# Conditioning rows of the first block: the matrix by rows in 8 KB lines, part of the contraction on DVE, the rest on PE

## The chip, the cores and the metric

The kernel runs on one core of one Trainium2 chip. The metric is the device time of one execution in microseconds (us), the median of three runs. A time "in the span" is counted from the first instruction of the profiled execution.

## What is computed

Three blocks of a network run one after the other over 512 tokens of width 1024. The change lies in the first step of the first block: a condition vector `c` of 1024 numbers goes through SiLU, is multiplied by a matrix `w_ada` of 1024 x 6144 (25.17 MB in float32), and a bias is added. The result is six rows of 1024 numbers, with which the tokens are shifted, scaled and gated:

```python
c_act = jax.nn.silu(c)                       # c: [1, 1024]
mod = c_act @ w_ada[l] + b_ada[l]            # w_ada: [1024, 6144], b_ada: [6144]
shift1, scale1, gate1, shift2, scale2, gate2 = jnp.split(mod, N_MOD, axis=-1)
h = modulate(rms_norm(x, norm1_g[l]), shift1, scale1)    # h * (1 + scale) + shift
...
x = x + gate1[:, None, :] * (merged @ w_out[l])
h2 = modulate(rms_norm(x, norm2_g[l]), shift2, scale2)
x = x + gate2[:, None, :] * peer(h2, ...)
```

All the rest (the mixers, the expert layer, the second and third block) stays as it is.

## The kernel before, in words

The program is a row of stages. `stage` (L42) opens a block in which each of the five engines runs its own list of instructions, ordered against the others by semaphores alone; at its end all engines meet (L45, L49) before the next stage begins. So nothing of the next stage starts before the slowest engine of this one is done.

`adaptive_rows` (L496) is the first real stage, called by `block_one` (L1104). The next one is the first norm of the tokens, whose first instruction on DVE (VectorE) is the BATCH_NORM_STATS of L399. The result of `adaptive_rows` is `mod`, six rows of 1024 numbers, each repeated on all 128 partitions.

- **Tiles.** The matrix is taken in 12 chunks of 512 columns. A chunk comes in two pieces of 1 MB (`kmajor`, L56), each with 4 of the 8 groups of 128 input rows: 128 partitions x 4 lines of 2 KB. A ring of `SLOTS` = 4 slots of 1 MB over the buffer `h_features` takes the 24 pieces.
- **SP** issues the pieces in order (L510), each after PE has used the slot's last piece, and then the first two 1 MB pieces of the next weights into `ring_raw` (L93).
- **ACT** (ScalarE) issues the load of `c` as a column (4 KB), the load of the bias repeated on all partitions straight into `mod` (3 MB written), computes SiLU, and after the 3rd and 6th chunk issues the loads of two gain rows (`row_a`, `row_b`, 0.5 MB each, repeated) and of the tokens `x` (2 MB).
- **PE** (TensorE) makes the product. `c_rep` holds SiLU(c) repeated over 128 columns, so that each of the 8 matmuls of a chunk (L536, 128x128 by 128x512, float32) adds up one group of 128 input rows, and the sum comes out alike on all 128 partitions. Two PSUM banks are used in turn. A float32 matmul shows as two records in the trace.
- **DVE** repeats SiLU(c) once (L545), adds each chunk's PSUM bank to `mod` (L551), and at the end forms (1 + scale) * gain for rows 1 and 4 (L555).

In the names of the trace `ada_ring` is the ring, `in_w_ada` the matrix in memory, `row_a` and `row_b` the gains, SPq and ACTq the DMA issues of an engine, PEq and DVEq an engine's sequencer (branches, drains).

Of the kernel before, what the change touches and what calls it, by code (L numbers as in the profile page):

```python
# [19 lines left out]
ALU = mybir.AluOpType  # L20
AX = mybir.AxisListType

P = 128
SEQ = 512
NT = SEQ // P
D = 1024
KD = D // P
BANK = 512
# [4 lines left out]
SLOTS = 4  # L33
# [461 lines left out]

def adaptive_rows(nc, core, d, mod, norm1_gain, norm2_gain):  # L496

    chunks = 6 * D // BANK
    pieces = [half for j in range(chunks) for half in kmajor(d["w_ada"][0], j * BANK, BANK)]
    ring = over(nc, core.hT_whole, "ada_ring", [P, SLOTS, PIECE])  # L500
    with buffers(nc, c_col=[P, KD], c_silu=[P, KD], c_rep=[P, KD, P]) as (c_col, c_silu, c_rep), \
            stage(nc, "ada", "c_loaded", "bias_loaded", "rest_loaded", "silu_done", "c_ready", "multiplied", "used", "evacuated",
                  *[f"landed{n}" for n in range(SLOTS)]) as (
                block, c_loaded, bias_loaded, rest_loaded, silu_done, c_ready, multiplied, used, evacuated, *landed):
        @block.sync
        def _(sp):
            for n, src in enumerate(pieces):
                if n >= SLOTS:
                    sp.wait_ge(used, n - SLOTS + 1)
                sp.dma_start(ring[:, n % SLOTS, :].rearrange("p (k n) -> p k n", k=KD // 2), src).then_inc(landed[n % SLOTS], 16)  # L510
            load_ahead(core, sp, core.splits + 2)

        @block.scalar
        def _(act):
            act.dma_start(c_col[:], d["c_col"]).then_inc(c_loaded, 16)
            act.dma_start(mod[:].rearrange("p a f -> p (a f)"), d["b_ada"][0, :].partition_broadcast(P)).then_inc(bias_loaded, 16)
            act.wait_ge(c_loaded, 16)
            nc.scalar.activation(c_silu[:], c_col[:], ACT.Silu).then_inc(silu_done, 1)
            act.wait_ge(multiplied, 3)
            act.dma_start(norm1_gain, d["norm1_g"][0, :].partition_broadcast(P)).then_inc(rest_loaded, 16)  # L520
            act.dma_start(norm2_gain, d["norm2_g"][0, :].partition_broadcast(P)).then_inc(rest_loaded, 16)
            act.wait_ge(multiplied, 6)
            act.dma_start(core.x[:], d["x"].rearrange("b (t p) f -> p (b t) f", p=P)).then_inc(rest_loaded, 16)

        @block.tensor
        def _(pe):
            pe.wait_ge(c_ready, 1)
            for c, turn, odd, _ in pairs(pe, 0, chunks):
                pe.wait_ge(evacuated, c + 1)
                for half in range(2):  # L530
                    slot = 2 * odd + half
                    pe.wait_ge(landed[slot], 16 * (turn + 1))
                    w = ring[:, slot, :].rearrange("p (k n) -> p k n", k=KD // 2)
                    for k in range(KD // 2):
                        kk = half * KD // 2 + k
                        mm = nc.tensor.matmul(core.ps[:, odd, :], c_rep[:, kk, :], w[:, k, :], start=kk == 0, stop=kk == KD - 1)  # L536
                    mm.then_inc(used, 1)
                    if half == 1:
                        pe.drain().then_inc(multiplied, 1)

        @block.vector
        def _(dve):
            dve.sem_inc(evacuated, 2)
            dve.wait_ge(silu_done, 1)
            nc.vector.tensor_copy(c_rep[:], c_silu[:].unsqueeze(2).to_broadcast([P, KD, P])).then_inc(c_ready, 1)  # L545
            dve.wait_ge(bias_loaded, 16)
            rows = mod[:].rearrange("p a f -> p (a f)")
            for j, _, odd, _ in pairs(dve, 0, chunks):
                dve.wait_ge(multiplied, j + 1)
# [1940 lines left out]
def column_tiles(v):  # L2490

    return np.ascontiguousarray(v.reshape(-1, P).T)
# [43 lines left out]
```

## Time and profile before

| | |
|---|---|
| median of 3 runs | 5344.36 us |
| lowest and highest of the 3 | 5342.21 and 5353.56 us |
| profiled execution, its own time | 5340.43 us |
| its span in the trace | 5338.6 us |
| start of the first norm's first DVE instruction in the span | 112.10 us |
| PE busy over the span | 4357.7 us (82%) |
| matrix loads of the stage | 24 of 1 MB |
| mean granted clock of PE over the span | 0.909 |

The granted clock (PEclk) is a share of full speed: 1.00 is the level of 2.4 GHz, 0.50 that of 1.2 GHz. "GB/s" is what all 16 DMA engines moved in a stretch. A timeline row has its start, its length, and in brackets how long the engine had been idle and what released it. The changed stage takes the first 112 us; the other stages have the same instructions before and after.

### The profile page before, as it was taken

How to read it: one execution, taken by the hardware profiler on the slowest of the kernel's cores; microseconds unless marked ns; L12 is line 12 of the kernel's file. 1: busy time of each engine (PE TensorE's matmuls, PEld its weight loads, DVE VectorE, ACT ScalarE, POOL GpSimd, SP SyncE). 2: the span in 40 equal slices, each digit the busy share in tenths (PEclk: the TensorE clock that was granted, in tenths of full speed). 3: DMA queues.
4: the chain of work that ended last, by engine and by line, in shares of the span. 5: the costliest groups of instructions: out<-in, count | busy, mean ns of one | idle time of the engine just before them, and what ended most of it. 6: DMA issues, size and time to landing. Idle time of an engine off the chain costs nothing. (4 is left out here: it accounts for less than half of the span.)

```text
span 5338.6 us, 46516 instructions
## 1 busy us (share of the span) xinstructions
PE 4357.7 (82%) x16256; PEld 2946.5 (55%) x16256; DVE 3132.0 (59%) x5411; ACT 731.9 (14%) x1680; POOL 818.7 (15%) x756
## 2 busy tenths in 40 slices
PE   7788969787787777677978678699996789787987
PEld 3676755222222222446746446577775567576876
DVE  2344357778778775654464485555556246445774
ACT  0111111111111010110131341100001210311000
POOL 1000023434433343100020041100002000001001
PEclk9899989999999999888989779799998699588998
DMA  7212216999999999200201101122222022022222
GB/s 252 85 56 81 88 63 260 423 424 423 423 416 416 415 416 421 76 24 8 75 16 64 49 1 53 60 87 89 91 90 68 24 75 80 8 73 74 95 77 75
DMA packets 212434, 813.26 MB, mean 152 GB/s; under 512 B 20288, under 2 KB 22608, under 8 KB 146448
## 3 DMA queue, kind: packets, MB, share of 16 engines
q0 software_dynamic: 73728, 536.90, 24.2%
q1 hardware_dynamic: 137408, 267.62, 15.1%
q10 hardware_dynamic: 1104, 6.30, 0.3%
q8 instruction: 104, 1.70, 0.1%
q14 instruction: 90, 0.74, 0.0%
HBM read 808.67 MB, written 2.10 MB: 152 GB/s over the span
## 5 line engine op out<-in xcount | busy, mean ns | idle before, releaser
L122 DVE CAST ring_high<-ring_raw 128x2048 fp32r<-128x2048 f32 (+2 forms) x250 | 274.4, 1097 | 934.7 <-PE psum L152 864.8
L150 PE MATMUL psum<-h_features,ring_high 128*128 128x512 f32 (+3 forms) x1432 | 566.0, 395 | 56.8 <-DVE ring_low L124 25.0
L151 PE MATMUL psum<-h_features,ring_high 128*128 128x512 f32 (+3 forms) x1432 | 562.4, 393 | 0.0
L152 PE MATMUL psum<-h_features,ring_low 128*128 128x512 f32 (+3 forms) x1432 | 562.0, 392 | 0.0
L124 DVE TENSOR_TENSOR ring_low<-ring_raw,ring_high 128x2048 fp32r<-128x2048 f32 (+2 forms) x250 | 509.6, 2038 | 19.0
L150 PE MATMUL psum<-ring_high,h_features 128*128 128x512 f32 x1120 | 443.1, 396 | 59.1 <-DVE ring_low L124 45.6
L925 PE MATMUL psum<-slots_ring,evacuation_tmp 128*128 128x512 f32 x816 | 403.7, 618 | 104.8 <-DVE evacuation_tmp L1023 104.7
L151 PE MATMUL psum<-ring_low,h_features 128*128 128x512 f32 x1120 | 441.0, 394 | 0.0
L152 PE MATMUL psum<-ring_high,h_features 128*128 128x512 f32 x1120 | 440.6, 393 | 0.0
L417 POOL TENSOR_SCALAR mean_var<-mean_var 128x1 f32<-128x1 f32 (+3 forms) x43 | 10.3, 241 | 2710.2 <-DVEq L455 1500.5
L925 PE MATMUL psum<-slots_features,evacuation_tmp 128*128 128x512 f32 x612 | 302.1, 617 | 77.2 <-DVE evacuation_tmp L1023 77.0
L925 PEld LDWEIGHTS psum<-slots_ring,evacuation_tmp 128*128 128x128 f32 x816 | 138.4, 189 | 369.0 <-DVE evacuation_tmp L1023 269.4
L150 PEld LDWEIGHTS psum<-h_features,ring_high 128*128 128x128 f32 (+3 forms) x1432 | 265.4, 185 | 130.0 <-issue 53.1
L1055 DVE CUSTOM_DVE_ANT_0 slots_ring<-slots_ring,h_tokens 128x1024 f32<-128x1024 f32 x204 | 249.8, 1225 | 101.5 <-DMA slots_ring<-in_peer_uv,expert 98.2
L152 PEld LDWEIGHTS psum<-h_features,ring_low 128*128 128x128 f32 (+3 forms) x1432 | 265.1, 185 | 64.4 <-issue 0.9
L151 PEld LDWEIGHTS psum<-h_features,ring_high 128*128 128x128 f32 (+3 forms) x1432 | 265.5, 185 | 62.5 <-issue 0.6
L150 PEld LDWEIGHTS psum<-ring_high,h_features 128*128 128x128 f32 x1120 | 213.6, 191 | 108.1 <-issue 48.3
L1096 ACT ACTIVATE weight<-score 128x1 f32<-128x1 f32 x512 | 103.9, 203 | 1131.9 <-DVE score L1055 1131.7
L872 POOL DMA_INDIRECT slots_ring<-in_peer_uv,expert x204 | 208.6, 1023 | 323.0 <-PE psum L925 291.2
L925 PEld LDWEIGHTS psum<-slots_features,evacuation_tmp 128*128 128x128 f32 x612 | 104.0, 189 | 274.2 <-DVE evacuation_tmp L1023 199.1
L925 PE MATMUL psum<-slots_mod,evacuation_tmp 128*128 128x512 f32 x416 | 207.5, 623 | 57.7 <-DVE evacuation_tmp L1023 57.6
L152 PEld LDWEIGHTS psum<-ring_high,h_features 128*128 128x128 f32 x1120 | 213.5, 191 | 45.1
(453 smaller groups left out, 7227.0 us busy)
## 6 DMA issues: line engine op xcount, KB each, us to landing
ring_raw<-in_w_in SPq DMA_DIRECT2D x94, 1024.0 KB, 5.0
ring_raw<-in_w_gate_up SPq DMA_DIRECT2D x32, 1024.0 KB, 5.1
ada_ring<-in_w_ada SPq DMA_DIRECT2D x24, 1024.0 KB, 5.9
ring_raw<-in_w_up_pairs SPq DMA_DIRECT2D x20, 1024.0 KB, 4.9
ring_raw<-in_w_down SPq DMA_DIRECT2D x33, 512.0 KB, 3.6
ring_raw<-in_w_out SPq DMA_DIRECT2D x12, 1024.0 KB, 5.0
ring_raw<-in_w_down SPq DMA_DIRECT2D x10, 1024.0 KB, 4.9
ring_raw<-in_peer_w_q SPq DMA_DIRECT2D x8, 1024.0 KB, 5.1
```

The costliest lines, as they stand in the source:

```text
L122: nc.vector.tensor_copy(high, whole)
L124: return nc.vector.tensor_tensor(low, whole, high.bitcast(F32), ALU.subtract)
L150: nc.tensor.matmul(out, a[0], b[0], start=start, stop=False)
L151: nc.tensor.matmul(out, a[0], b[1], start=False, stop=False)
L152: return nc.tensor.matmul(out, a[1], b[0], start=False, stop=stop)
L417: nc.gpsimd.tensor_scalar(v, v, eps, None, ALU.add).then_inc(done, 1)
L872: nc.gpsimd.indirect_dma_start(out=slots[slot_of[n]], out_offset=None, in_=rows, in_offset=bass.IndirectOffsetOnAxis(ap=expert[:, t, i:i + ...
L925: mm = nc.tensor.matmul(banks(t)[q], diagonal[:, n % DIAGONALS, :], slots[slot_of[n]][:, D + q * BANK:D + (q + 1) * BANK], start=i == 0, s ...
L1055: nc.vector.tensor_tensor_reduce(out=u, in0=u, in1=core.h[:, t, :], scale=1.0, scalar=0.0, op0=ALU.mult, op1=ALU.add, accum_out=score[:, i ...
L1096: nc.scalar.activation(weight[:, i:i + 1], score[:, i:i + 1], ACT.Gelu).then_inc(activated, 1)
```

## The change

The matrix is laid out anew in memory (`laid_out`): first by the six rows of the result, then by quarters of the contraction, then by partition. A piece is now 128 partitions x one line of 8 KB: 2 groups of 128 input rows by all 1024 columns of one row of `mod`. There are again 24 pieces of 1 MB, 4 for each row of `mod`, in the order of rows 1, 4, 0, 2, 3, 5. The ring has 8 slots, 4 over `h_features` and 4 over `ring_high` and `ring_low`.

Of the 4 pieces of a row, DVE takes the first three: 6 instructions of 128x1024 that multiply a group by its SiLU(c), a number per partition, and add it to `sums`. Each waits by a drain for the one before. PE takes the fourth piece as before (4 matmuls against `c_rep`), adds the bias by 2 matmuls over one partition of ones, and adds the 128 partitions of `sums` by 2 matmuls against a block of ones. So 8 matmuls remain for a row instead of 16. Rows 1 and 4 are brought from PSUM by DVE with their gain in one instruction each; the other four by a copy on ACT. The bias is loaded as one line of 24 KB, and the gains and `x` are issued by ACT after the first row's sums.

```diff
+ADA_ORDER = (1, 4, 0, 2, 3, 5)
+ADA_PIECES, ADA_SUMMED = 4, 3
...
         @block.sync
         def _(sp):
-            for n, src in enumerate(pieces):
-                if n >= SLOTS:
-                    sp.wait_ge(used, n - SLOTS + 1)
-                sp.dma_start(ring[:, n % SLOTS, :].rearrange("p (k n) -> p k n", k=KD // 2), src).then_inc(landed[n % SLOTS], 16)
+            for i, r in enumerate(ADA_ORDER):
+                for q in range(ADA_PIECES):
+                    if i >= turns:
+                        if q < ADA_SUMMED:
+                            sp.wait_ge(used_summed, ADA_SUMMED * (i - turns) + q + 1)
+                        else:
+                            sp.wait_ge(used_direct, i - turns + 1)
+                    sp.dma_start(ring(i, q), d["w_ada_rows"][r, q].rearrange("p (k n) -> p k n", k=2)).then_inc(landed_at(i, q)[0], 16)
             load_ahead(core, sp, core.splits + 2)
...
         def _(act):
-            act.dma_start(mod[:].rearrange("p a f -> p (a f)"), d["b_ada"][0, :].partition_broadcast(P)).then_inc(bias_loaded, 16)
+            act.dma_start(bias[:], d["b_ada"]).then_inc(bias_loaded, 16)
...
-            act.wait_ge(multiplied, 3)
+            act.wait_ge(summed, 1)
...
+            for i, r in enumerate(ADA_ORDER):
+                if r not in gains:
+                    act.wait_ge(multiplied, i + 1)
+                    nc.scalar.copy(mod[:, r, :].rearrange("p (b n) -> p b n", b=2), core.ps[:, bank(i):bank(i) + 2, :]).then_inc(copied, 1)
+            act.wait_ge(x_loaded, 16)
...
         def _(pe):
...
-                        mm = nc.tensor.matmul(core.ps[:, odd, :], c_rep[:, kk, :], w[:, k, :], start=kk == 0, stop=kk == KD - 1)
...
+                if i >= 4:
+                    pe.wait_ge(gained, gained_at[i - 4] + 1)
...
+                    nc.tensor.matmul(out[half], ones[0:1, :], bias[:, r * D + half * BANK:r * D + (half + 1) * BANK], start=True, stop=False)
+                pe.wait_ge(*landed_at(i, ADA_SUMMED))
+                for k in range(2):
+                    for half in range(2):
+                        mm = nc.tensor.matmul(out[half], c_rep[:, k, :], ring(i, ADA_SUMMED)[:, k, cols[half]], start=False, stop=False)
+                mm.then_inc(used_direct, 1)
+                pe.wait_ge(summed, i + 1)
+                for half in range(2):
+                    mm = nc.tensor.matmul(out[half], ones[:], sums[:, i % 2, cols[half]], start=False, stop=True)
+                mm.then_inc(multiplied, 1)
...
         def _(dve):
-                nc.vector.tensor_tensor(part, part, core.ps[:, odd, :], ALU.add).then_inc(evacuated, 1)
...
+            for i, r in enumerate(ADA_ORDER):
+                if i >= 2:
+                    dve.wait_ge(multiplied, i - 1)
+                total = sums[:, i % 2, :]
+                for q in range(ADA_SUMMED):
+                    dve.wait_ge(*landed_at(i, q))
+                    for k in range(2):
+                        c = c_silu[:, 2 * q + k:2 * q + k + 1]
+                        if q + k == 0:
+                            done = nc.vector.tensor_scalar(total, ring(i, q)[:, k, :], c, None, ALU.mult)
+                        else:
+                            dve.drain()
+                            done = nc.vector.scalar_tensor_tensor(total, ring(i, q)[:, k, :], c, total, ALU.mult, ALU.add)
+                    done.then_inc(used_summed, 1)
+                    if q == 0 and i - 1 in gained_at:
+                        gain(i - 1)
+                dve.drain().then_inc(summed, 1)
```

On DVE, at the start of `adaptive_rows`, the program had this (the two L551 rows are the body of a loop that runs 6 times):

```order
L545 COPY c_rep<-c_silu 128x1024
L170 UNCONDITIONAL_BRANCH
L170 ISA
L551 ISA
L551 TENSOR_TENSOR mod<-mod,psum 128x512
L549 REGISTER_ALU
L551 ISA
L551 TENSOR_TENSOR mod<-mod,psum 128x512
L170 REGISTER_ALU
L170 COMPARE_AND_BRANCH
L555 SCALAR_TENSOR_TENSOR mod<-mod,row_a 128x1024
L555 SCALAR_TENSOR_TENSOR mod<-mod,row_b 128x1024
```

And has this now (`ada_features` and `ada_ring` are the two halves of the ring; L591 and L594 are the products, L577 the rows with a gain):

```order
L581 COPY c_rep<-c_silu 128x256
L591 TENSOR_SCALAR sums<-ada_features_83,c_silu 128x1024
L594 SCALAR_TENSOR_TENSOR sums<-ada_features_83,c_silu,sums 128x1024 x5
L591 TENSOR_SCALAR sums<-ada_ring_84,c_silu 128x1024
L594 SCALAR_TENSOR_TENSOR sums<-ada_ring_84,c_silu,sums 128x1024
L577 SCALAR_TENSOR_TENSOR mod<-psum,row_a 128x1024
L594 SCALAR_TENSOR_TENSOR sums<-ada_ring_84,c_silu,sums 128x1024 x4
L591 TENSOR_SCALAR sums<-ada_features_83,c_silu 128x1024
L594 SCALAR_TENSOR_TENSOR sums<-ada_features_83,c_silu,sums 128x1024
L577 SCALAR_TENSOR_TENSOR mod<-psum,row_b 128x1024
```

DVE has 36 products instead of 12 additions, and the two gains stand inside the second and third row instead of at the end.

On PE the same place, before (a loop of 6 turns, 16 matmuls each):

```order
L532 ISA
L536 MATMUL psum<-ada_ring_83,c_rep 128x512 x8
L529 REGISTER_ALU
L536 MATMUL psum<-ada_ring_83,c_rep 128x512 x8
L170 REGISTER_ALU
L170 COMPARE_AND_BRANCH
```

And now (the first two of six rows; L560 is the bias, L564 the fourth piece, L568 the sum over partitions):

```order
L560 MATMUL psum<-bias,ones 128x512 x2
L564 MATMUL psum<-ada_features_83,c_rep 128x512 x4
L568 MATMUL psum<-sums,ones 128x512 x2
L560 MATMUL psum<-bias,ones 128x512 x2
L564 MATMUL psum<-ada_ring_84,c_rep 128x512 x4
L568 MATMUL psum<-sums,ones 128x512 x2
```

PE has 48 matmuls in the stage instead of 96, written out without a loop; those of L568 stand behind DVE's sums.

## Rows read from the trace of the kernel before

**Rows 1.** the page, its head: engine, busy us, share of the span, instructions.
```profile
PE 4357.7 (82%) x16256; PEld 2946.5 (55%) x16256; DVE 3132.0 (59%) x5411; ACT 731.9 (14%) x1680; POOL 818.7 (15%) x756
```
**Rows 2.** busy time by stretch; last three columns: PEclk, DMA share, GB/s.
```profile
50.00:60.00 10.00, 9.60 (x23) 4.08 (x22) 0.69 (x1) 0.00 (x0) 0.00 (x0) 1.00 0.93 300
80.00:90.00 10.00, 9.60 (x23) 4.02 (x23) 0.69 (x1) 0.00 (x0) 0.00 (x0) 1.00 0.87 300
```
**Rows 3.** waits of the first 145 us: engine, line, releaser: us, times, longest.
```profile
DVE mod L551 <- PEq L539: 93.6, 12, 16.9
PE psum L536 <- DMA ada_ring<-in_w_ada: 12.9, 2, 8.3
PE psum L536 <- issue: 6.0, 11, 0.7
```
**Rows 4.** by line, first 160 us: busy us, mean ns of one.
```profile
L536 PE MATMUL psum<-ada_ring,c_rep 128*128 128x512 f32 x192 | 89.1, 618 | 18.9 <-DMA ada_ring<-in_w_ada 12.9 <-issue 6.0
L551 DVE TENSOR_TENSOR mod<-mod,psum 128x512 f32 x12 | 8.2, 687 | 93.6 <-PEq L539 93.6
```
**Rows 5.** timeline, end of the stage: start us, us, engine, line, operation.
```profile
100.88 7.11 PE L536 MATMUL psum<-ada_ring,c_rep 128*128 128x512 f32 x16 [0.40 <-issue]
108.17 0.69 DVE L551 TENSOR_TENSOR mod<-mod,psum 128x512 f32 x1 [6.82 <-PEq L539]
108.97 1.22 DVE L555 SCALAR_TENSOR_TENSOR mod<-mod,row_a 128x1024 f32<-128x1024 f32 x1
112.10 1.29 DVE L399 BATCH_NORM_STATS2 bn_parts<-x_tokens 128x6 f32<-128x512 f32 x2 [0.76 <-PEq L49]
```
**Rows 6.** DMA issues, first 200 us: KB each, median us to landing.
```profile
ada_ring<-in_w_ada SPq DMA_DIRECT2D x24, 1024.0 KB, 5.9
ring_raw<-in_w_in SPq DMA_DIRECT2D x8, 1024.0 KB, 5.2
x_tokens<-in_x ACTq DMA_DIRECT2D x1, 2048.0 KB, 10.9
```
**Rows 7.** busy time by stretch, for the DMA rate in the last column.
```profile
3.00:5.00 2.00, 0.00 (x0) 0.00 (x0) 0.00 (x0) 1.28 (x1) 0.00 (x0) 1.00 0.62 128
8.00:12.00 4.00, 3.66 (x5) 1.62 (x6) 0.00 (x0) 0.00 (x0) 0.00 (x0) 1.00 1.00 426
16.00:18.00 2.00, 0.00 (x0) 0.00 (x0) 0.00 (x0) 0.00 (x0) 0.00 (x0) 1.00 1.05 397
1000.00:1100.00 100.00, 78.59 (x160) 26.95 (x160) 78.77 (x197) 13.70 (x46) 40.06 (x40) 1.00 1.01 424
1900.00:2000.00 100.00, 78.66 (x160) 26.75 (x158) 76.04 (x189) 10.71 (x42) 40.77 (x40) 1.00 1.01 414
```
**Rows 8.** groups by line and form on DVE, whole span.
```profile
L318 DVE SCALAR_TENSOR_TENSOR evacuation_tmp<-psum,taps,evacuation_tmp 128x511 f32<-128x511 f32 x21 | 15.8, 750 | 3.4 <-issue 3.4
L1222 DVE TENSOR_SCALAR y<-y,mean_var 128x128 f32<-128x128 f32 x32 | 6.4, 287 | 6.1 <-POOL mean_var L419 6.1
L1222 DVE TENSOR_SCALAR y<-y,mean_var 128x256 f32<-128x256 f32 x16 | 4.3, 350 | 3.5 <-POOL mean_var L419 3.5
L1055 DVE CUSTOM_DVE_ANT_0 slots_ring<-slots_ring,h_tokens 128x1024 f32<-128x1024 f32 x204 | 249.8, 1225 | 101.5 <-DMA slots_ring<-in_peer_uv,expert 98.2
```
**Rows 9.** timeline on PE, and PEclk by stretch behind two of the gaps.
```profile
18.34 5.40 PE L536 MATMUL psum<-ada_ring,c_rep 128*128 128x512 f32 x8 [4.57 <-DMA ada_ring<-in_w_ada]
...
4392.71 0.50 PE L150 MATMUL psum<-ring_high,yT 128*128 128x512 f32 x1 [3.33 <-DVEq L243]
...
4393.00:4396.40 3.40, 3.40 (x16) 2.74 (x16) 3.32 (x2) 0.00 (x0) 0.00 (x0) 1.00 0.02 5
...
2765.42 1.79 PE L1649 MATMUL psum<-q_tile,far 128*128 128x128 f32 x11 [3.60 <-DVE far L1556]
...
2765.70:2769.00 3.30, 3.30 (x21) 3.30 (x20) 2.97 (x5) 0.00 (x0) 0.00 (x0) 0.61 0.03 7
```
**Rows 10.** groups by line and form on ACT, whole span.
```profile
L2212 ACT COPY y<-psum 128x1024 f32<-128x1024 f32 x4 | 4.0, 1014 | 7.9 <-PE psum L2205 7.9
```

More of the change, by code:

```diff
@@ L32 @@
 PIECE = KD // 2 * BANK
-SLOTS = 4
 ALPHA = 2.0 ** 0.25
@@ L493, with _ @@
 SGU_GROUPS, SGU_DIM = 4, 256
+ADA_ORDER = (1, 4, 0, 2, 3, 5)
+ADA_PIECES, ADA_SUMMED = 4, 3
 def adaptive_rows(nc, core, d, mod, norm1_gain, norm2_gain):
[L498 to L504, printed above, removed]
+    turns = 2
+    gains = {1: norm1_gain, 4: norm2_gain}
+    gained_at = {i: n for n, i in enumerate(i for i, r in enumerate(ADA_ORDER) if r in gains)}
+    in_features = over(nc, core.hT_whole, "ada_features", [P, ADA_PIECES, 2, D])
+    in_ring = over(nc, core.high, "ada_ring", [P, ADA_PIECES, 2, D])
+    ring = lambda i, q: (in_features, in_ring)[i % turns][:, q]
+    with buffers(nc, c_col=[P, KD], c_silu=[P, KD], c_rep=[P, 2, P], ones=[P, P], sums=[P, 2, D], bias=[1, 6 * D]) as (
+            c_col, c_silu, c_rep, ones, sums, bias), \
+            stage(nc, "ada", "c_loaded", "bias_loaded", "gains_loaded", "x_loaded", "ones_ready", "silu_done", "c_ready", "used_summed", "used_direct",
+                  "summed", "multiplied", "copied", "gained", *[f"landed{n}" for n in range(turns * ADA_PIECES)]) as (
+                block, c_loaded, bias_loaded, gains_loaded, x_loaded, ones_ready, silu_done, c_ready, used_summed, used_direct,
+                summed, multiplied, copied, gained, *landed):
+        bank = lambda i: 2 * (i % 4)
+        landed_at = lambda i, q: (landed[ADA_PIECES * (i % turns) + q], 16 * (i // turns + 1))
+        @block.gpsimd
+        def _(pool):
+            nc.gpsimd.memset(ones[:], 1.0).then_inc(ones_ready, 1)
@@ L527, in _ @@
             pe.wait_ge(c_ready, 1)
-            for c, turn, odd, _ in pairs(pe, 0, chunks):
-                pe.wait_ge(evacuated, c + 1)
-                for half in range(2):
[L531 to L535, printed above, removed]
-                        mm = nc.tensor.matmul(core.ps[:, odd, :], c_rep[:, kk, :], w[:, k, :], start=kk == 0, stop=kk == KD - 1)
-                    mm.then_inc(used, 1)
-                    if half == 1:
-                        pe.drain().then_inc(multiplied, 1)
+            pe.wait_ge(bias_loaded, 16)
@@ L541, in _ @@
         @block.vector
         def _(dve):
-            dve.sem_inc(evacuated, 2)
-            dve.wait_ge(silu_done, 1)
[L545 to L549, printed above, removed]
-                part = rows[:, bass.ds(j * BANK, BANK)]
-                nc.vector.tensor_tensor(part, part, core.ps[:, odd, :], ALU.add).then_inc(evacuated, 1)
@@ L552, in _, with gain @@
-            dve.drain()
-            dve.wait_ge(rest_loaded, 48)
-            for which, gain in ((1, norm1_gain), (4, norm2_gain)):
-                nc.vector.scalar_tensor_tensor(mod[:, which, :], mod[:, which, :], 1.0, gain, ALU.add, ALU.mult)
+            def gain(i):
+                r = ADA_ORDER[i]
+                dve.wait_ge(gains_loaded, 32)
+                dve.wait_ge(multiplied, i + 1)
+                nc.vector.scalar_tensor_tensor(mod[:, r, :].rearrange("p (b n) -> p b n", b=2), core.ps[:, bank(i):bank(i) + 2, :], 1.0,
+                                               gains[r].rearrange("p (b n) -> p b n", b=2), ALU.add, ALU.mult).then_inc(gained, 1)
```

13 lines of the change are left out of this document (9 added, 4 removed).

## The prediction

> **What bounds the kernel now.** I read the page's head first: PE is busy 4357.7 us of the span, 82% [rows 1]. That share is an average over the whole program; the change touches only the first 112 us, so I read that stretch alone. By stretches of 10 us, PE is busy 9.60 at a granted clock of 1.00, DVE 0.69, and the DMA engines move 300 GB/s [rows 2]. The waits say who is late: DVE waits 93.6 us for PE, while PE waits 12.9 us for the matrix, all of it in the first 19 us, and 6.0 us at the turn of chunks [rows 3]. So the stage is bound by PE: 192 records of 618 ns [rows 4], 16 of them (8 matmuls) in 7.11 us for a chunk [rows 5], which is 0.89 us for a float32 matmul at the 2.4 GHz level. The reader should see that the DMA engines, at 300 GB/s, are held back by the ring: a slot comes free only when PE has used it. Behind the last chunk stand DVE's addition and two gain instructions of 1.22 us, then 0.76 us of meeting, and the norm starts at 112.10 [rows 5]. The stages end in a meeting of all engines, so whatever this stage gives back moves the start of the norm by just that much.
>
> **The change, part by part.**
>
> *PE's matmuls.* 16 per row of `mod` become 8: 8 x 0.89 = 7.1 us for a row at 2.4 GHz, 43 us in all. PE stops being the bound if a row takes longer elsewhere.
>
> *DVE's products.* The trace has no 128x1024 product with a number per partition whose operands all lie in SBUF. Nearest: the gain instruction, 1.22 us [rows 5]; and at 128x511 the form with a number per partition takes 750 ns [rows 8], where an addition of two tensors over 512 takes 687 [rows 4], 0.06 more. So 1.28 us, and 0.10 for the drain, as between the end of L551 (108.17 + 0.69) and the next start (108.97) [rows 5]: 1.38. The first product of a row has one tensor only: 287 ns for 128 elements and 350 for 256 [rows 8], so 0.063 per 128 and about 0.73 for 1024, with its drain 0.85. A row costs DVE 0.85 + 5 x 1.38 = 7.75 us, 46.5 in all, and 2 x 1.3 for the gains. Does DMA at full rate slow DVE? A 128x1024 instruction in the gather stage takes 1225 ns [rows 8] beside 424 GB/s [rows 7]: no. Bounds of a product: 1.22 and 1.6.
>
> *DMA.* A row is four pieces, 4.19 MB. At what rate? Three rows bear on it. The 2 KB lines of this stage, with the ring not yet full, came at 397 GB/s; mixed with the 24 KB lines of the bias, 426; the gather of 8 KB lines later in the kernel at 424, and at 414 in a worse stretch [rows 7]. The new lines are 8 KB, so I take 424: 9.9 us for a row. That is more than PE's 7.1 and DVE's 7.75, so **the bound moves to DMA**. Eight slots hold 20 us of transfers ahead, which covers DVE's wait for the gains in the second row (they are issued only after the first row's sums) and the clock of PE.
>
> On this the Trainium skill speaks against the change: "DMA: Bandwidth & Descriptors" (section on bandwidth, "Where 436 GB/s comes from") says that for loads from memory the memory side, about 358 GB/s for a core, binds. The trace disagrees: 424 GB/s held for 100 us [rows 7]. By the page's figure, an estimate, the bytes below would take 78.4 us instead of 66.2, and the gain would be 19.7 us.
>
> *The end of the loads.* All bytes: 24 pieces 25.17 MB, `x` 2.10, gains 1.05, bias 0.02: 28.34 MB. The 3 MB of the repeated bias are gone. The first 2 us (3 to 5) moved 128 GB/s [rows 7], 0.26 MB. The remaining 28.08 MB at 424 GB/s take 66.2 us: last byte at 71.2. Between last byte and landing: a lone 1 MB lands 5.2 us after its issue [rows 6], of which 2.6 are its bytes at 397 GB/s. Of the other 2.6, before the first byte and behind the last, I put 0.8 behind (bounds 0 and 2.6). The last piece lands at **72.0**. The two pieces into `ring_raw` are issued behind it on the same queue; nobody needs them before the norm is over, so they cost nothing.
>
> *The tail.* The last piece of each row is PE's. DVE gets its third piece 2.5 us earlier and needs 2.8, so its sums are ready 0.3 to 0.7 us after the last landing, under PE's 4 direct matmuls (3.6 us). Then 2 matmuls for the sum: 6 x 0.89 = 5.3 us at 2.4 GHz, 10.7 at 1.2. Which? PE will have idled some 9.9 - 7.1 = 2.8 us before it. In the trace a gap of 4.57 us was followed by a stretch at half clock (8 records in 5.40 us instead of 3.6); one of 3.60 us by a mean clock of 0.61, one of 3.33 by 1.00 [rows 9]. So I add half the loss of the middle case: 0.9. Tail: 6.2. Then 0.2 to the reader (107.99 to 108.17), ACT's copy of 128x1024 from PSUM, 1.01 [rows 10], and the meeting, 0.76 [rows 5]. DVE has nothing behind PE's last matmul any more: its two gains are done in the rows before.
>
> **Sum:** 72.0 + 6.2 + 0.2 + 1.0 + 0.8 = 80.2, against 112.10: **31.9 us less**. Everything after is the same program. Against the profiled execution, 5340.4 - 31.9 = 5308.5; the median of the runs lies 3.9 above that execution, so 5344.4 - 31.9 = **5312.5**, which I give. The later stages' clock steps fall differently against the work once it all starts 32 us earlier; that may move the total by a few us either way.
>
> **The rivals.**
>
> 1. *The lines are served no better than 2 KB ones.* 28.08 MB at 397 GB/s take 70.7 us, 4.5 more; at 386, as low as such a mix might fall, 6.5 more: 5317 to 5319. For it: a load by the SP queue is not the gather. Against: the rate rises with the line in rows 7, 397 to 424 and 426. Chance 0.13.
> 2. *The queue serves its transfers together, not in turn.* Then the row's four pieces land at once, and with the two for `ring_raw`: landing 5 us later (2.1 MB at 424) and DVE's 7.75 us behind it instead of beside it, with 1.8 for the sum. The norm starts near 72.0 + 5.0 + 7.75 + 1.8 + 2.0 = 88.5: 5321. Against: a median of 5.9 us to landing for 1 MB with others under way [rows 6]. Chance 0.09.
> 3. *PE stays the bound at a low clock.* With 2.8 us idle in each row the clock could stay at the 1.2 GHz level: 14.2 us for a row. From the first row's end near 15 + 10.7, five more: 96.8, norm at 98.8, 5331. Against: at 14.2 us a row PE would no longer idle, and in steady work rows 2 show 1.00; behind the gap of 4.57 us the slow records had an end too, since all 8 took 5.40 us and not 7.1 [rows 9]. Chance 0.05.
> 4. *The memory side binds below the rate of rows 7.* This core would then stay between the 300 GB/s of rows 2 and 397. Midway, at 350, the 28.08 MB take 80.2 us, 14.0 more, and the gain is 17.9: 5326.5. Chance 0.03. At 300 they take 93.6 us, the norm starts at 107.6 and the gain is 4.5 us, no measurable change: chance 0.02. Against both: 424 GB/s over 100 us [rows 7].
>    This is the mechanism of the Trainium skill's sentence above; with its 358 GB/s, an estimate again, the time would be 5324.7.
> 5. *Slower: the transfers do not overlap.* If each waited for the one before to land, 24 x 5.2 us [rows 6] = 125 us; norm near 135.5, 23 us later: 5368. It decides from 4.2 us per transfer on: (112.1 - 2.3 - 8.2) / 24. Against: 397 GB/s in rows 7 with several queued, where a lone one has 1 MB in 5.2 us, 202 GB/s. Chance 0.02.
>
> **How the numbers follow.** The forecast has 0.66, and its own bounds are: rate 414 to 430 (2 us later, 1 earlier), tail 5.3 to 10.7 (1 earlier, 4.5 later), a product of 1.6 us (DVE's row 9.3, still under 9.9; less than 1 us on the tail), and some 5 us for the clock steps of later stages: 5303 to 5321. The range reaches on over rivals 1 and 2 with a few us of the same clock steps: 5302 to 5326, with 0.12 left out (rivals 3, 4 and 5) beside the forecast's own ends. About 0.2% or 11 us is what a measurement of this kernel can tell from no change. The forecast, rivals 1, 2, 3 and rival 4 at 350 GB/s all gain 13 us or more: 0.66 + 0.13 + 0.09 + 0.05 + 0.03 = 0.96 faster; 0.02 same (rival 4 at 300); 0.02 slower (rival 5).
>
> **What would show it.** Right: the norm's first DVE instruction near 80 us; 410 to 425 GB/s in the stretches between 10 and 70 us; PE's waits in the stage now for the ring, and DVE's for the ring, not for PE; products of about 1.28 us. Rival 1 shows as 390 GB/s, rival 2 as landings of 10 us and more with DVE's six products bunched at the end, rival 3 as PEclk near 0.5 from 20 to 90 us. The forecast is wrong if the norm starts early but the total does not follow, or if the products take over 1.7 us, where DVE's row passes 9.9 us and becomes the bound.

## The result, and the profile after

The changed kernel takes 5316.76 us in the median of 6 runs (5312.19 to 5324.9), the kernel before 5346.85 in 6 runs beside it: ratio 0.9945, with a 95% interval of 0.9933 to 0.9957, or 30 us less. Timed a second time, it was 5322.0 us (5 runs) against 5339.8 (11 runs): ratio 0.9966, interval 0.9952 to 0.9979, 18 us less. Both intervals lie below 1, so the kernel is faster, by 0.55% and 0.34% in the medians. The forecast was 5312.5 with a range of 5302 to 5326. Both medians lie in it; the second gain is little more than half of the one forecast, and where the rest went is told below. (The first 3 of the 6 runs of before are those of the table ahead.)

The changed stage itself did nearly what was forecast. The page's head and the first 110 us in stretches, as [rows 1] and [rows 2] (the last three columns are PEclk, the DMA share and GB/s):

```profile
PE 4341.9 (82%) x16160; PEld 2939.7 (55%) x16160; DVE 3162.5 (59%) x5435; ACT 736.6 (14%) x1684; POOL 825.5 (16%) x757
30.00:70.00 40.00, 33.46 (x60) 12.69 (x58) 31.87 (x28) 2.02 (x2) 0.00 (x0) 0.79 1.01 422
52.00:62.00 10.00, 9.18 (x17) 3.45 (x16) 7.24 (x7) 1.01 (x1) 0.00 (x0) 0.83 1.01 421
```

The DMA engines now run full, 422 GB/s over 40 us at a share of 1.01, where [rows 2] had 300. DVE is busy 7.2 us of the 10 from 52 to 62 and PE 9.2, at a clock of 0.83, where I had expected 7.1 us of work for each 9.9. Over the 40 us PE is busy 33.5, at 0.79: part of its busy time is the slower clock.

The waits of the stage, against [rows 3] (engine, line, releaser, then us in total, times, longest): each engine that works on the matrix now waits for the matrix.

```profile
DVE mod L577 <- DMA row_b<-in_norm_g: 8.8, 1, 8.8
PE psum L560 <- DMA bias<-in_b_ada: 8.4, 1, 8.4
PE psum L564 <- DMA ada_features<-in_w_ada_rows: 7.7, 3, 3.5
PE psum L564 <- DMA ada_ring<-in_w_ada_rows: 5.3, 3, 3.5
DVE sums L591 <- DMA ada_ring<-in_w_ada_rows: 5.2, 3, 2.1
```

The groups of the stage, against [rows 4] and [rows 8] (busy us, mean ns of one): a product of DVE takes 1284 ns, the first of a row 753.

```profile
L594 DVE SCALAR_TENSOR_TENSOR sums<-ada_ring,c_silu,sums 128x1024 f32<-128x1024 f32 x15 | 19.3, 1284 | 1.8 <-DMA ada_ring<-in_w_ada_rows 0.7
L591 DVE TENSOR_SCALAR sums<-ada_ring,c_silu 128x1024 f32<-128x1024 f32 x3 | 2.3, 753 | 5.2 <-DMA ada_ring<-in_w_ada_rows 5.2
L564 PE MATMUL psum<-ada_ring,c_rep 128*128 128x512 f32 x24 | 16.8, 869 | 5.3 <-DMA ada_ring<-in_w_ada_rows 5.3
```

And the end of the stage in time, against [rows 5]: the last row of `mod`, from DVE's first product to the norm.

```profile
65.46 0.75 DVE L591 TENSOR_SCALAR sums<-ada_ring,c_silu 128x1024 f32<-128x1024 f32 x1 [2.06 <-DMA ada_ring<-in_w_ada_rows]
67.95 5.38 DVE L594 SCALAR_TENSOR_TENSOR sums<-ada_ring,c_silu,sums 128x1024 f32<-128x1024 f32 x4 [0.37 <-DMA ada_ring<-in_w_ada_rows]
69.97 1.98 PE L560 MATMUL psum<-bias,ones 1*128 1x512 f32 x4
72.87 5.40 PE L564 MATMUL psum<-ada_ring,c_rep 128*128 128x512 f32 x8 [0.93 <-DMA ada_ring<-in_w_ada_rows]
78.11 1.88 PE L568 MATMUL psum<-sums,ones 128*128 128x512 f32 x4
80.03 1.01 ACT L546 COPY mod<-psum 128x1024 f32<-128x1024 f32 x1 [8.94 <-PE psum L568]
81.89 1.29 DVE L398 BATCH_NORM_STATS2 bn_parts<-x_tokens 128x6 f32<-128x512 f32 x2 [8.56 <-PEq L48]
```

DVE is done with its six products at 73.33, while PE has only begun its last four matmuls at 72.87, when their piece landed. They take 5.24 us, at first at full clock and then, from 74 to 77 us, at half (0.51 and 0.50). The norm starts at 81.89 instead of 112.10: 30.2 us earlier.

### The profile page after: what moved, and what is told of

It reads as the page before. It is cut to its first block and busy times, and to the rows that moved or that the text cites. A ratio compares the mean times of both kernels' runs of the same rounds, so it can differ in the third digit from the quotient of the medians.

```text
span 5318.9 us, 46309 instructions
## 1 busy us (share of the span) xinstructions
PE 4341.9 (82%) x16160; PEld 2939.7 (55%) x16160; DVE 3162.5 (59%) x5435; ACT 736.6 (14%) x1684; POOL 825.5 (16%) x757
## 5 line engine op out<-in xcount | busy, mean ns | idle before, releaser
L123 DVE TENSOR_TENSOR ring_low<-ring_raw,ring_high 128x2048 fp32r<-128x2048 f32 (+2 forms) x250 | 509.5, 2038 | 19.8 <-issue 1.0
```

The costliest lines, as they stand in the source:

```text
L123: return nc.vector.tensor_tensor(low, whole, high.bitcast(F32), ALU.subtract)
```

## The experiments

In each diff the lines are those of the changed kernel with `+` and `-` against it. "The norm" is the start of its first instruction on DVE; the stretches are those of each kernel's own trace. Experiments 1 to 10 are one profiled execution each, so they are read by their traces and not by their totals: single totals of the kernel before alone range from 5328.45 to 5355.74 us. Those of experiments 3 to 10, in the order of their numbers, are 5326.76, 5340.34, 5326.57, 5299.51, 5321.64, 5321.68, 5314.75 and 5321.39 us. Experiments 5 and 6 leave out part of the product.

**1 and 2. Both kernels once more, unchanged.**

> The kernel before once more, unchanged, to see what moves by itself. In the two profiled executions the changed kernel starts the norm 30.2 us earlier but ends its span only 19.7 us earlier; 8.7 us of the difference lie in the gated linear attention stage of the second block (from the load of w in in_gla_w to the load of in_gla_norm: 205.1 us before, 213.8 after) where PE's granted clock is 0.85 against 0.81. Theory A (that stage's clock falls by chance of timing, in either kernel): norm again at 112.1 us within 0.5, total within 5342 to 5356, and this stage not fixed at 205.1 but anywhere in 204 to 215. Theory B (the change itself slows that stage): norm at 112.1 and the stage again at 205.1 within 1 us.

> The changed kernel once more, unchanged. Theory A (chance of the clock): norm at 81.9 us within 0.5, total 5312 to 5325, the gated linear attention stage anywhere in 204 to 215 us. Theory B (the change slows that stage): norm at 81.9 and that stage again at 213.8 within 1 us.

The norm started at 110.98 us in the kernel before (1.12 earlier, where 0.5 was allowed) and at 80.51 in the changed one (1.38 earlier): 30.5 us apart, as the first pair. Totals were 5335.28 and 5312.82, the first under its range too. The attention stage took 206.4 us and 210.6. Theory B (205.1 and 213.8, within 1 us) missed both. Theory A allowed anything from 204 to 215, so it holds both without being shown by them. The passage behind experiment 12 comes back to it.

The changed kernel's tail shows what the norm's 1.4 us are: here the clock was full, and the last direct matmuls took 3.5 us instead of 5.2. A row earlier it had been low: PE idled 2.58 us, and the direct matmuls took 6.5.

```profile
60.00:70.00 10.00, 7.42 (x11) 3.07 (x11) 7.25 (x7) 0.00 (x0) 0.00 (x0) 0.66 1.01 421
62.86 6.71 PE L564 MATMUL psum<-ada_features,c_rep 128*128 128x512 f32 x8 [2.58 <-DMA ada_features<-in_w_ada_rows]
73.12 3.70 PE L564 MATMUL psum<-ada_ring,c_rep 128*128 128x512 f32 x8
80.51 1.28 DVE L398 BATCH_NORM_STATS2 bn_parts<-x_tokens 128x6 f32<-128x512 f32 x2 [7.25 <-PEq L48]
```

The changed kernel thus has at least two courses. In the three stretches of 10 us from 50 to 80 the clock was 0.83, 0.83 and 0.83 in the first execution, and 1.00, 0.66 and 1.00 here and again in experiment 12 (norm at 80.41). An experiment's norm is therefore to be held against 80.4 to 81.9, and against one end of that only where the tail took the same course.

**3. The matrix in lines of 2 KB.**

```diff
-    ...reshape(KD // 2, 2, P, 6, D).transpose(3, 0, 2, 1, 4)).reshape(6, KD // 2, P, 2 * D)
+    ...reshape(KD // 2, 2, P, 6, 2, BANK).transpose(3, 0, 1, 4, 2, 5)).reshape(6, KD // 2, 4, P, BANK)
-                    sp.dma_start(ring(i, q), d["w_ada_rows"][r, q].rearrange("p (k n) -> p k n", k=2))
+                    sp.dma_start(ring(i, q).rearrange("p k (h n) -> p (k h) n", h=2), d["w_ada_rows"][r, q].rearrange("a p n -> p a n"))
```

> The changed kernel with one thing undone: the matrix comes in lines of 2 KB (4 lines a partition in each 1 MB piece) instead of one line of 8 KB; split between DVE and PE, ring, order and bytes stay. Theory 1 (the stage is bound by the stream, and the rate follows the line): the 28.08 MB at 395 instead of 423 GB/s take 4.7 us more, the norm starts at 86.6 us, the stretches between 30 and 70 us show 385 to 400 GB/s. Rival (the line does not matter, the split gave all): norm at 81.9 within 0.5, 420 GB/s. Rival (the line gave most of the gain): norm past 100 us.

```profile
50.00:60.00 10.00, 8.01 (x15) 2.96 (x14) 6.99 (x7) 1.01 (x1) 0.00 (x0) 0.77 1.05 387
78.23 5.95 PE L564 MATMUL psum<-ada_ring,c_rep 128*128 128x512 f32 x8 [3.52 <-DMA ada_ring<-in_w_ada_rows]
```

387 GB/s at a full share, the last piece 5.4 us later (78.23 against 72.87), the norm at 87.80, 5.9 later than in the first execution; the other 0.5 us are slower direct matmuls. Theory 1 holds, with a rate at its lower edge: the line of 8 KB is worth 5 to 6 us of the 30.

**4. All of the product on PE, with the new layout, ring and loads.**

```diff
-                pe.wait_ge(*landed_at(i, ADA_SUMMED))
...
+                for q in range(ADA_PIECES):
+                    pe.wait_ge(*landed_at(i, q))
+                    for k in range(2):
+                        for half in range(2):
+                            mm = nc.tensor.matmul(out[half], c_rep[:, 2 * q + k, :], ring(i, q)[:, k, cols[half]], start=False, stop=2 * q + k == KD - 1)
```

> The changed kernel with DVE's part given back to PE: new layout, 8 KB lines, 8 slots, bias by matmul and late gains stay; all four pieces of a row are multiplied on PE (16 matmuls and 2 for the bias), no sums on DVE. Theory 1 (PE was the bound, and the split freed the stream): 108 matmuls at 0.89 us are 96 us behind the first landing near 8.4, so the norm starts at 106 to 109 us, DMA falls to about 270 GB/s between 30 and 90 us, PE is over 9.5 of 10 us busy at clock 1.00. Rival (layout and ring gave the gain): norm at 82 to 88 us.

```profile
60.00:70.00 10.00, 9.89 (x23) 4.00 (x22) 0.00 (x0) 1.01 (x1) 0.00 (x0) 1.00 0.68 242
80.00:90.00 10.00, 10.00 (x21) 4.20 (x20) 0.00 (x0) 0.00 (x0) 0.00 (x0) 0.83 0.73 286
45.88 15.70 PE L562 MATMUL psum<-ada_features,c_rep 128*128 128x512 f32 x32
63.59 14.00 PE L562 MATMUL psum<-ada_ring,c_rep 128*128 128x512 f32 x32
114.90 1.29 DVE L398 BATCH_NORM_STATS2 bn_parts<-x_tokens 128x6 f32<-128x512 f32 x2 [69.70 <-PEq L48]
```

PE is never idle from 8.36 us on, DMA falls to 242 to 286 GB/s, and the norm starts at 114.90, later than in the kernel before and 6 us above my bound: the product of a row takes 14.0 us in two rows and 15.7 or 15.8 in four, since the clock dipped there although PE had no gap. With all of the product on PE nothing is gained, so the gain needs the split, which frees the stream. That layout, ring and late gains are worth nothing by themselves is not shown: this kernel also has 12 matmuls for the bias on PE, 10.7 us at 0.89 each, about as much as PE's idle time shrank (18.9 us in [rows 4], 8.4 here).

**5. Half of DVE's products left out.**

```diff
-                    for k in range(2):
+                    for k in range(1):
                         c = c_silu[:, 2 * q + k:2 * q + k + 1]
```

> The changed kernel with half of DVE's products left out: of each of its pieces only the first group of 128 input rows is multiplied (18 instructions instead of 36), so the second, fourth and sixth eighth of the contraction are missing from the result. Loads and PE's work stay. Theory 1 (the stream is the bound and DVE hides under it): norm at 81.9 us within 0.5. Rival (DVE's chain of drained products is the bound): 18 products of 1.38 us less, 25 us, norm at 60 to 70 us as far as the stream allows, with the stream above 430 GB/s. DVE's wait for the gains in the second row stays.

```profile
30.00:70.00 40.00, 33.37 (x60) 12.77 (x58) 14.21 (x13) 2.02 (x2) 0.00 (x0) 0.79 1.02 422
81.92 1.29 DVE L398 BATCH_NORM_STATS2 bn_parts<-x_tokens 128x6 f32<-128x512 f32 x2 [10.17 <-PEq L48]
```

DVE 14.2 us busy instead of 31.9 in the same 40 us, the stream at the same 422 GB/s, the norm at 81.92. The execution took the course of the first one (clock 0.83 in the tail), and its norm lies within 0.03 us of it: DVE's work is hidden.

**6. A quarter of the matrix less.**

```diff
-                for q in range(ADA_PIECES):
+                for q in (0, 1, 3):
...
-                for q in range(ADA_SUMMED):
+                for q in range(2):
```

> The changed kernel without the third piece of each row: neither loaded nor multiplied (6 of 24 pieces, 6.29 MB; the fifth and sixth eighth of the contraction are missing). DVE has 4 products a row, PE its 8 matmuls. Theory 1 (stream bound at 423 GB/s): 14.9 us less, norm at 67.0 us, if PE at 7.4 us of stream a row does not take over: its 8 matmuls are 7.1 us at clock 1.00 and more at the mean clock 0.83 now seen (about 8.6), in which case 6 rows of 8.6 from 15 us on give 67 to 70. Rival (PE or DVE bound now): norm at 78 us or later.

```profile
40.00:50.00 10.00, 9.64 (x19) 3.46 (x17) 6.59 (x6) 1.01 (x1) 0.00 (x0) 0.83 1.01 421
59.14 3.70 PE L564 MATMUL psum<-ada_ring,c_rep 128*128 128x512 f32 x8
66.45 1.29 DVE L398 BATCH_NORM_STATS2 bn_parts<-x_tokens 128x6 f32<-128x512 f32 x2 [8.42 <-PEq L48]
```

The norm at 66.45: 15.4 us less than in the first execution, where 6.29 MB at 422 GB/s are 14.9. That the two agree so well is partly luck: the last direct matmuls start only 13.7 us earlier (59.14 against 72.87), and the other 1.7 us are their full clock; against the executions with a full clock in the tail the norm gains 14.0. PE is 9.64 us of 10 busy here and works without a gap from 42.93 on, so its last direct matmuls did not wait for their piece. With 3.15 MB or 7.5 us of stream for a row, PE and not the stream sets the pace of the last two rows.

**7 and 10. PE kept busy between rows,** first with a second pair of bias matmuls over one partition, then with the same length of work over all partitions.

```diff
-                for half in range(2):
-                    nc.tensor.matmul(out[half], ones[0:1, :], bias[...], start=True, stop=False)
+                for stop in (True, False):
+                    for half in range(2):
+                        nc.tensor.matmul(out[half], ones[0:1, :], bias[...], start=True, stop=stop)
```

```diff
+                for half in (0, 1, 0, 1):
+                    nc.tensor.matmul(out[half][:, 0:2 * P], ones[:], c_rep[:].rearrange("p a n -> p (a n)"), start=True, stop=True)
```

> The changed kernel with two more matmuls a row on PE: the bias pair is done twice, the first time into the same banks and then overwritten, while PE would wait for the matrix; result unchanged. It asks whether PE's short idle time between rows (2.8 us of 9.9) costs clock in the tail. Now PEclk is 0.83 in each row, the last 4 direct matmuls take 5.24 us (72.87 to 78.11) instead of 3.6. Theory 1 (idling cost 1.7 us in the tail): with 8.9 us of work in 9.9, PEclk 1.00 between 50 and 80 us, last direct matmuls in 3.6 us, norm at 80.2. Rival (the clock falls all the same, or the additional work makes PE late): norm at 81.9 or later, up to 83.7.

> What fell in e7 was the clock in spite of a busy PE: over 9.9 of 10 us busy, PEclk 0.83 and 0.75, and the direct matmuls behind the four bias matmuls over one partition took 5.2 to 6.5 us instead of 3.6. Here the additional work has the same length (about 1.8 us a row), but as four matmuls over all 128 partitions and 256 columns; result unchanged. Theory C (it is the matmuls over one partition, not idle time, behind which the clock falls): with full-height work beside them PEclk is 0.95 or more between 50 and 80 us, the last direct matmuls take 3.6 to 3.8 us and the norm starts at 80 to 81 us. Theory D (the additional work as such makes PE late): norm at 84 to 86 us as in e7, PEclk 0.75 to 0.85.

Stretches of 10 us and the end of each kernel's stage in time: above the dots experiment 7, below them 10:

```profile
50.00:60.00 10.00, 10.00 (x20) 3.81 (x19) 7.24 (x7) 1.01 (x1) 0.00 (x0) 0.83 1.02 419
70.00:80.00 10.00, 10.00 (x18) 3.75 (x17) 4.33 (x4) 1.01 (x1) 0.00 (x0) 0.75 0.74 280
71.99 4.24 PE L561 MATMUL psum<-bias,ones 1*128 1x512 f32 x8
76.16 6.51 PE L565 MATMUL psum<-ada_ring,c_rep 128*128 128x512 f32 x8
86.28 1.29 DVE L398 BATCH_NORM_STATS2 bn_parts<-x_tokens 128x6 f32<-128x512 f32 x2 [11.71 <-PEq L48]
...
50.00:60.00 10.00, 10.00 (x30) 5.23 (x29) 6.39 (x6) 1.77 (x2) 0.00 (x0) 1.00 1.01 419
60.00:70.00 10.00, 8.94 (x20) 3.73 (x19) 7.24 (x7) 0.26 (x1) 0.00 (x0) 0.83 1.02 424
70.00:80.00 10.00, 10.00 (x27) 4.57 (x25) 4.06 (x4) 1.01 (x1) 0.00 (x0) 1.00 0.73 278
74.58 3.70 PE L566 MATMUL psum<-ada_ring,c_rep 128*128 128x512 f32 x8
81.90 1.29 DVE L398 BATCH_NORM_STATS2 bn_parts<-x_tokens 128x6 f32<-128x512 f32 x2 [7.59 <-PEq L48]
```

In experiment 7 PE is busy 10.00 us of 10 and the clock is 0.83 and 0.75; the last direct matmuls, behind four of the bias, take 6.5 us, and the norm starts at 86.28, 4.4 later than in the changed kernel. So PE had not idled before the clock fell: my theory of the tail, in the prediction and in this expectation, is refuted as far as idle time is its whole cause. In experiment 10 the clock is 1.00 in two of three stretches and 0.83 in the third, and the last direct matmuls take 3.5 us, but they start 1.7 us late behind the added work: 81.90. Theory C's 0.95 missed, and neither edit buys time. Nor do the two separate the theories: 1.00, a low stretch and 1.00 is also the course of the unchanged kernel in experiments 2 and 12. More telling for matmuls over one partition is experiment 4: without a gap ahead of them three of its six rows ran 1.7 us slow behind such a pair, and the kernel before, which has none, shows 1.00 in every stretch of 10 us from 30 to 100. But two rows of experiment 4 did not slow down, and no run took the bias off PE, so it is not shown.

**8. PE's piece first in each row.**

```diff
-                for q in range(ADA_PIECES):
+                for q in (3, 0, 1, 2):
```

> The changed kernel with the order of the pieces in each row turned: PE's piece is loaded first, DVE's three behind it. Theory (the tail is what follows the last landing): behind it now stand 4 matmuls and 2 more (5.24 and 1.9 us); then it is 2 products of 1.38 us and a drain, 2.9, and 2 matmuls of 1.8 to 2.7 after an idle time: norm at 79.0 to 80.5 us, 1.5 to 3 us earlier. Rival (DVE is too late with its pieces, for each row now needs 7.7 us of it in the last 7.4 us of the stream): norm at 81.9 or later.

```profile
69.86 3.70 PE L564 MATMUL psum<-ada_ring,c_rep 128*128 128x512 f32 x8
75.96 1.99 PE L568 MATMUL psum<-sums,ones 128*128 128x512 f32 x4 [2.40 <-DVEq L598]
79.84 1.29 DVE L398 BATCH_NORM_STATS2 bn_parts<-x_tokens 128x6 f32<-128x512 f32 x2 [3.98 <-PEq L48]
```

The direct matmuls are over at 73.6, PE waits 2.4 us for DVE's sums, and the norm starts at 79.84, 2.1 us earlier than in the first execution and within the expectation, but only 0.6 us earlier than in the executions whose tail also had the full clock (80.51 and 80.41). So the order of the last pieces is worth 0.6 to 2.1 us.

**9. The tokens behind the matrix,** issued by SP and no longer by ACT.

```diff
                     sp.dma_start(ring(i, q), ...).then_inc(landed_at(i, q)[0], 16)
+            sp.dma_start(core.x[:], d["x"].rearrange("b (t p) f -> p (b t) f", p=P)).then_inc(x_loaded, 16)
...
-            act.dma_start(core.x[:], d["x"].rearrange("b (t p) f -> p (b t) f", p=P)).then_inc(x_loaded, 16)
```

> The changed kernel with the load of the tokens x (2.10 MB) moved from ACT's queue, where it runs beside the second and third row of the matrix, to SP's queue behind the last piece of the matrix. Theory 1 (the stage is bound by what the stream moves before the last piece): 2.10 MB at 423 GB/s less ahead of it, 5.0 us; the last direct matmuls start at 67.9 instead of 72.87 and the norm at 75.5 to 77.0 us; x lands near 73 under the tail. Rival (the stream has slack, or x is now late): norm at 79 us or later.

```profile
67.58 5.33 PE L564 MATMUL psum<-ada_ring,c_rep 128*128 128x512 f32 x8 [1.13 <-DMA ada_ring<-in_w_ada_rows]
76.53 1.29 DVE L398 BATCH_NORM_STATS2 bn_parts<-x_tokens 128x6 f32<-128x512 f32 x2 [8.49 <-PEq L48]
```

The last piece is in use at 67.58 instead of 72.87 and the norm starts at 76.53: 5.4 us for 2.10 MB moved out of the way, with a tail of the same course (5.2 us for the last direct matmuls in both); 2.10 MB at 422 GB/s are 5.0. Together with experiments 3 and 5 this shows that the stage goes at the pace of the stream. PE is close behind: in experiments 2 and 12 its last direct matmuls no longer waited for their piece.

**11. The edits of experiments 8 and 9 together, timed, and 12. the changed kernel timed beside it.**

> The changed kernel with both edits that paid: PE's piece first in each row (e8: norm at 79.84 instead of 81.89, 2.1 us) and x behind the matrix (e9: 76.53, 5.4 us). If the stream is the bound up to its last piece and the tail follows it, the two add up: norm at 74.0 to 75.0 us, and the time falls by 7 us against the changed kernel, 37 us (0.7%) against the kernel before, ratio 0.993. Rival (x, which lands near 73 us, now holds up the end of the stage through ACT's wait): norm at 75 to 76 us. Rival (what the stage gives is lost later to the clock of the gated linear attention stage): norm at 74.5 but no gain over the changed kernel in the time.

> The changed kernel, unchanged, timed on the same chip as e11 for the comparison of the two: ratio to the kernel before 0.9935 to 0.9955 (30 us). Norm at 80.5 to 81.9 us. If the gated linear attention stage costs the changed kernel 4 to 9 us in every execution, the ratio lies near 0.996 instead.

```profile
45.00:50.00 5.00, 3.63 (x9) 1.12 (x7) 4.54 (x5) 0.00 (x0) 0.00 (x0) 1.00 0.75 265
30.75 1.23 DVE L577 SCALAR_TENSOR_TENSOR mod<-psum,row_a 128x1024 f32<-128x1024 f32 x1 [8.32 <-DMA row_b<-in_norm_g]
37.56 3.55 PE L568 MATMUL psum<-sums,ones 128*128 128x512 f32 x4 [11.64 <-DVEq L598]
76.57 1.29 DVE L398 BATCH_NORM_STATS2 bn_parts<-x_tokens 128x6 f32<-128x512 f32 x2 [3.98 <-PEq L48]
```

The two edits did not add up. The norm starts at 76.57, 2 us later than the sum of them would give (74.5). The row of the stretch 45 to 50 us shows where: 265 GB/s at a share of 0.75, so the stream paused. 5 us at 265 instead of 422 GB/s are 0.79 MB, or 1.9 us, and that is the 2. What stopped it is a slot that came free late. The trace has the chain: DVE waits 8.32 us for the gains in the second row (the changed kernel has this too, 8.8), its sums are late, PE waits 11.64 us for them, so its direct matmuls of the third row run from 42.95 to 46.65, and at 46.68 SP issues the piece that goes into their slot. Experiment 8 has the same chain, but there the stream still had the tokens to move, and it stayed at 419 GB/s from 45 to 50 us. No run took the wait for the gains away, so that this would give the 2 us back is argued and not shown. It is neither rival that I had written down. The medians: 5318.68 us (6 runs, 5301.68 to 5324.1), ratio 0.9960 (0.9947 to 0.9974), against 5322.0 and 0.9966 (0.9952 to 0.9979) for the changed kernel: no difference that this timing can tell. The profiled execution of experiment 11, 5301.68 us, is the fastest of its six, 17 us under their median.

**Where the rest of the time goes.** In its three profiled executions the norm of the changed kernel starts 29 to 32 us before those of the kernel before, but the totals give less: the first profiled pair (5340.43 and 5320.66) lies 19.8 us apart where the norms lie 30.2, and experiments 1 and 2 lie 22.5 apart where the norms lie 30.5. The gated linear attention stage of the second block, whose instructions are the same in all of them, takes these times (the stretch of the row, from the load of `in_gla_w` to that of `in_gla_norm`; in order: before, before in experiment 1, after, experiment 11; its columns are those of the stretches above):

```profile
2628.27:2833.39 205.12, 167.33 (x732) 115.02 (x732) 110.00 (x147) 59.30 (x138) 41.77 (x33) 0.86 0.08 24
2625.39:2831.75 206.36, 168.55 (x732) 118.02 (x732) 109.90 (x147) 59.30 (x138) 41.66 (x33) 0.85 0.08 24
2596.92:2810.74 213.82, 176.81 (x732) 121.58 (x732) 106.88 (x147) 59.30 (x138) 42.08 (x33) 0.82 0.08 23
2585.31:2787.67 202.36, 167.01 (x732) 115.03 (x732) 109.80 (x147) 59.31 (x138) 42.70 (x33) 0.86 0.08 25
```

205.1, 206.4, 213.8 and 202.4 us. The busy time of ACT and POOL is alike; PE has the same 732 records, and is busy 167 to 169 us at a clock of 0.85 or 0.86, 177 at 0.82. The stage is slower where the clock is lower. Over all profiled executions it took 205.1 to 206.4 us in the kernel before (two executions) and with all of the product on PE (once), 209.5 to 213.9 in ten of those with the split, and 202.4 in experiment 11. So part of the gain is given back there in ten of eleven profiled executions with the split, by 3 to 9 us: of the 10.4 us that the first pair lost behind the norm, 8.7 are this stage. (Experiments 1 and 2: 4.3 of 8.0.) The rest lies in later stages that I did not separate. Two profiled executions of the kernel before are few, however. Over all runs of the first timing the medians lie 30.1 us apart, as far as the norms do; the first pair lies closer because the kernel before was profiled 6.4 us under its median and the changed one 3.9 over its own. How long the stage takes in the runs without a trace is not known. It is not a fixed price of the change: the same kernel had 210.6 and 213.8, experiment 11 had the least of all (in the fastest of its six runs), and experiments 4 and 11 differ from the changed kernel in the first 115 us alone. What in those first microseconds decides how the clock falls 2.5 ms later stays open; I have no run that separates it.

## Why the prediction came out as it did

- **What bounds the kernel before.** Right: PE. Experiment 4 puts its work back and the stage is again as long as before and a little longer (114.90 against 112.10), with PE never idle.
- **DVE's products.** Forecast 1.28 us and 0.73, measured 1.284 and 0.753; a row takes 7.87 us (65.46 to 73.33) against 7.75. The end of the stage does not wait for it (experiment 5).
- **The stream.** Forecast 424 GB/s, measured 422; the last piece was to land at 72.0 and PE was released by it at 72.87. The 422 holds for 30 to 70 us; from 5 to 72 us the trace has 419, since the stretch from 20 to 30 came at 402. At 419 the 28.08 MB take 0.8 us more than at 424. The first 2 us (3 to 5) moved 214 GB/s and not 128, which is worth 0.4 us the other way. The remaining 0.5 I can't place: the landing, for which I had put 0.8 with bounds of 0 and 2.6, is not to be read by itself. Rival 1 is what experiment 3 builds: 2 KB lines come at 387 GB/s, within the 386 to 397 of its price, and cost 5.9 us where 4.5 to 6.5 were worked out. The Trainium skill's 358 GB/s ("DMA: Bandwidth & Descriptors", section on bandwidth, "Where 436 GB/s comes from") does not bind here: the matrix itself came at 422. I had read that passage alone: ahead of it the same section of the Trainium skill gives about 358 GB/s as what each core gets when both cores of a pair stream, and this kernel runs on one core; no run here has two.
- **The tail.** This term was mis-sized, and its reason was at best half right. Forecast 6.2 us; measured 7.1 in the profiled execution (72.87 to 79.99) and 5.4 in the other two (73.12 to 78.54 in experiment 2). So 6.2, a loss halved for not knowing, lies between two courses, and that it is close to their middle is luck. I had PE idle 2.8 us in each row. In the first execution it was busy 9.2 us of 10 in the last rows at a clock of 0.83, and the gap ahead of the last direct matmuls was 0.93 us; in experiments 4 and 7 the clock fell with no gap. In experiments 2 and 12 a gap of 2.6 us did precede the slow direct matmuls of the fifth row, as I had reasoned, and PE then had no gap, and the full clock, ahead of the last ones. Rival 3 has a grain of truth in it: PE at this clock is nearer to the bound than I thought, as experiment 6 shows.
- **Behind the tail.** Copy 1.01 as forecast, the way to it 0.04 instead of 0.2, the meeting 0.85 instead of 0.76.
- **The sum.** 80.2 forecast; 81.89, 80.51 and 80.41 measured in the three profiled executions of the changed kernel. A gain of 31.9 us in the stage was forecast; 30.2 and 30.5 measured in the two pairs. The kernel before moved too: its norm started at 112.10 and at 110.98.
- **"Everything after is the same program."** The instructions are, the time is not. I allowed 5 us for the clock steps of later stages; the attention stage alone moved by up to 8.7 between the two profiled executions I compare, so this term was too small for a single execution. That the second timing (18 us) falls short for the same reason is likely and not shown, since the runs of a timing leave no trace.
- **The total.** The median of 5316.76 is 4.3 above the forecast. Of this, 2.5 are the kernel before, whose median is 5346.85 over six runs and was 5344.36 over the three that I had. The gain, 30.1 by the medians, is 1.8 short of the 31.9, and the stage's own gain was short by 1.7 in the first pair. In the second timing the gain is 14 short, and I can't say by which stage. My own sign of a wrong forecast, a norm that starts early with a total that does not follow, is thus met in part there (18 us of about 30) and in the first profiled pair (19.8 of 30.2).
- **The bounds.** The widths that I gave my own terms (2 us later or 1 earlier for the rate, 4.5 or 1 for the tail, under 1 for the products, 5 either way for later stages) add up to 5305.5 and 5325, not to the 5303 and 5321 that I wrote. The range of 5302 to 5326 covers both.
- **Signs I had named.** "Landings of 10 us and more" was a poor sign for rival 2: the median landing is 16 us simply because eight transfers stand in the queue, and the pieces still arrive in turn:

```profile
ada_features<-in_w_ada_rows SPq DMA_DIRECT2D x12, 1024.0 KB, 16.2
55.55 0.75 DVE L591 TENSOR_SCALAR sums<-ada_features,c_silu 128x1024 f32<-128x1024 f32 x1 [2.08 <-DMA ada_features<-in_w_ada_rows]
58.02 5.38 DVE L594 SCALAR_TENSOR_TENSOR sums<-ada_features,c_silu,sums 128x1024 f32<-128x1024 f32 x4 [0.35 <-DMA ada_features<-in_w_ada_rows]
```

  DVE waits 2.08 us for the first piece of a row and 0.35 for the second; bunched landings would show one long wait and six products without any.

## What to carry to other kernels

When an engine that multiplies a vector by a large matrix is the bound and the loads run below the rate seen elsewhere in the same trace, move work off it until the stream is full, and stop there: from then on only bytes ahead of the last piece and the work behind it count (2.10 MB moved back: 5.4 us; the order of the last pieces: 0.6 to 2.1 us). Price a load by the rows of the trace with the same line length, not by a rate per core. Profile the same kernel more than once before a difference of 1 or 2 us is put down to an edit: here the norm of the changed kernel moved by 1.5 us by itself. And check a gain of half a percent against the stages that did not change: here one of them moved by up to 8.7 us, where the gain was 18 to 30.

## What was not expected of the hardware

- The granted clock of PE fell to 0.83 and 0.75 in stretches with PE busy 10.00 us of 10 (experiment 7), where each row held four matmuls over a single partition, and in experiment 4 it fell in three of six rows, behind two such matmuls and with no gap of PE ahead. A gap is therefore not needed for the clock to fall; whether the matmuls over one partition are what lowers it is open. Two float32 matmuls over one partition, four records, take 1.98 us, as long as two over all 128 (1.88 to 1.99).
- The changed kernel's first stage has two courses without any edit: the clock from 50 to 80 us was 0.83, 0.83, 0.83 once and 1.00, 0.66, 1.00 twice, and the norm moved by 1.5 us with it.
- The same attention stage with the same instructions takes 202.4 to 213.9 us, with granted clocks of 0.86 to 0.82; 210.6 and 213.8 come back to the tenth in several executions, so it looks like a few courses rather than a spread.
- The rate of a load from memory goes with its line at a full share of the engines: 387 GB/s with 2 KB (experiment 3), 422 with 8 KB.
